# A paired-head recurrence on one core: the next pair's key projection moved behind the second inverse level, and one VectorE operation per chunk step

## The reference, cut to what matters

```python
zs = z + (jnp.pad(z, ((0, 0), (1, 0), (0, 0)))[:, :S] - z) * mu     # token shift
r, k, v, wd, ad, gd = _split(zs, ...)
w = -jax.nn.softplus(-(w0 + jnp.tanh(wd) @ w2)) - 0.5
decay = jnp.exp(-jnp.exp(w)); iclr = jax.nn.sigmoid(a0 + ad @ a2); g = jax.nn.sigmoid(gd) @ g2
kk = heads(k * k_k); kk = kk / jnp.maximum(jnp.sqrt(jnp.sum(kk * kk, -1)), 1e-12)
k = k * (1.0 + (iclr - 1.0) * k_a)
# per head, for each token:
#   sa = state @ a_t                       with a = -kk, b = kk * iclr
#   state = state * w_t + sa b_t^T + v_t k_t^T
#   y_t = state @ r_t
y = groupnorm(y) * gn_w + gn_b
bonus = jnp.sum(rh * kh * r_k, -1) * vh
out = (y + bonus) * g
```

## Time and profile before

| | us |
|---|---|
| median of three executions | 4002.56 |
| lowest, highest | 4001.58, 4009.13 |
| profiled execution | 4011.43 |
| its span, first to last instruction | 4009.6 |
| granted TensorE clock, mean | 0.984 |

### The profile page before, as it was taken

One profiled execution on the slowest core, in us unless ns is written; L12 is line 12 of the kernel. 1 busy time (PEld: TensorE's weight loads), 2 busy tenths in 40 slices (PEclk: granted clock), 3 DMA queues, 4 the chain that ended last, 5 costly groups with the idle time before them and its releaser, 6 DMA issues.

```text
span 4009.6 us, 68639 instructions
## 1 busy us (share of the span) xinstructions
PE 3778.5 (94%) x28412; PEld 3042.1 (76%) x28412; DVE 2020.4 (50%) x3578; ACT 1698.7 (42%) x2505; POOL 800.9 (20%) x1120
## 2 busy tenths in 40 slices
PE   7989999998999999989999999998999999999997
PEld 5777788777778877877777788876777777778885
DVE  4585651247553127356663476225645565357603
ACT  3475332346533237455553332235744544342223
POOL 1112222211222221200001222221120000222221
PEclk9999999999999999999999999999999999999998
DMA  9946998984699975733324889986583222779896
GB/s 306 232 97 141 278 243 188 234 216 106 137 208 194 192 171 114 178 86 69 69 61 98 176 189 192 193 176 143 114 183 74 54 63 53 158 172 192 191 193 139
DMA packets 191750, 628.90 MB, mean 157 GB/s; under 512 B 22992, under 2 KB 28368, under 8 KB 191056
## 3 DMA queue, kind: packets, MB, share of 16 engines
q0 software_dynamic: 160704, 549.53, 63.0%
q1 hardware_dynamic: 28176, 70.79, 5.1%
q10 hardware_dynamic: 2560, 4.20, 0.4%
HBM read 612.89 MB, written 2.10 MB: 153 GB/s over the span
## 4 chain that ended last, share of the span: by engine, by line
PE 51%; DVE 6%; DMA 3%; ACT 2%; issue 1%; SPq 0%; POOL 0%; DVEq 0%; ACTq 0%
PE bank L229 13%; PE bank L231 12%; PE bank L230 12%; PE bank L2091 4%; PE bank L2054 1%; DVE rw_z L2552 1%; PE bank L1772 1%; PE bank L1754 1%; PE bank L1745 1%; PE bank L2080 1%; DMA at_sw<-at_raw 1%; ACT gate L2280 1%; DMA w_lo<-in_b_wup 1%; DVE x L398 0%; PE bank L2068 0%
## 5 line engine op out<-in xcount | busy, mean ns | idle before, releaser
L229 PE MATMUL bank<-h_hi,w_hi 128*128 128x512 f32 x2608 | 1066.8, 409 | 25.8 <-DMA w_lo<-in_a_wgv 6.4
L231 PE MATMUL bank<-h_hi,w_lo 128*128 128x512 f32 x2608 | 1023.7, 393 | 0.0
L230 PE MATMUL bank<-h_lo,w_hi 128*128 128x512 f32 x2608 | 1023.1, 392 | 0.0
L162 ACT ACTIVATE w_lo<-w_hi 128x1024 fp32r<-128x1024 f32 (+2 forms) x558 | 557.6, 1003 | 1034.0 <-DMA w_hi<-in_a_wgv 292.7
L229 PEld LDWEIGHTS bank<-h_hi,w_hi 128*128 128x128 f32 x2608 | 493.8, 189 | 166.1 <-issue 52.5
L230 PEld LDWEIGHTS bank<-h_lo,w_hi 128*128 128x128 f32 x2608 | 494.1, 189 | 106.3 <-issue 11.5
L231 PEld LDWEIGHTS bank<-h_hi,w_lo 128*128 128x128 f32 x2608 | 493.4, 189 | 106.9
L2280 ACT ACTIVATE gate<-bank 128x512 f32<-128x512 f32 x96 | 57.3, 597 | 230.6 <-PE bank L2091 228.4
L1509 DVE TENSOR_SCALAR fa_conv<-fa_a_in,par_a 128x512 f32<-128x512 f32 x44 | 22.3, 507 | 228.9 <-ACT fa_a_in L1449 228.5
L229 PE MATMUL bank<-fa_y_hi,w_hi 128*128 128x512 f32 x352 | 137.1, 390 | 0.4 <-DMA w_lo<-in_a_wd 0.4
L229 PE MATMUL bank<-fb_y_hi,w_hi 128*128 128x512 f32 x352 | 137.0, 389 | 0.4 <-DMA w_lo<-in_b_wd 0.4
(11 more groups left out here) (466 smaller groups left out, 7505.0 us busy)
## 6 DMA issues: line engine op xcount, KB each, us to landing
w_hi<-in_a_wgv POOLq DMA_DIRECT2D x80, 512.0 KB, 5.3
w_lo<-in_a_wgv POOLq DMA_DIRECT2D x80, 512.0 KB, 7.6
w_hi<-in_b_wup POOLq DMA_DIRECT2D x80, 512.0 KB, 5.0
w_lo<-in_b_wup POOLq DMA_DIRECT2D x80, 512.0 KB, 7.4
w_hi<-in_a_wh POOLq DMA_DIRECT2D x48, 512.0 KB, 5.6
w_lo<-in_a_wh POOLq DMA_DIRECT2D x48, 512.0 KB, 5.6
w_hi<-in_b_wrkv POOLq DMA_DIRECT2D x48, 512.0 KB, 4.3
w_lo<-in_b_wrkv POOLq DMA_DIRECT2D x48, 512.0 KB, 5.4
```

What stands on the lines that cost most here:

```text
L162: st.do(st.eng.activation(self.lo[:, s], self.hi[:, s].bitcast(F32), ACT.Copy, scale=-1.0), (self.neg_made, n + 1))
L229: pe.matmul(out, self.hi[:, a], hh[:, k0 + k, :], start=first and k == 0, stop=False)
L230: pe.matmul(out, self.hi[:, a], hl[:, k0 + k, :], start=False, stop=False)
L231: mm = pe.matmul(out, self.lo[:, a], hh[:, k0 + k, :], start=False, stop=last and k == ks - 1)
```

## The change

Pieces change their place in the lists of the three engines; no operation is added or removed.

- PE: the k unit of pair p+1 stands in one piece behind `inverse_t(p, 1)` and its chunk step; the decay matmuls of pair p+1 stand in the last level, behind `lower(p, 4)` and its step. `dense(p)` begins with r; `ssq` stands behind its second block (behind its sixth in pair 0), the variance behind its fifth. The bonus matmul and `scores(p, 1)` stand behind `scores(p, 0)`, ahead of the four-way scores, each with chunk steps around them. The upper four-way products go to bank 4 instead of 3.
- ACT: the squares of the keys follow the decays; `keep_y` follows them; the variance's logarithm follows that of the key norm, so that both use one table load; k is copied in level 2 of the pair ahead. The weights of the pieces are negated in the same order, three calls at other places.
- DVE: the key shift stands in the pair ahead, between steps 21 and 22; `post` behind `at`; step 0 ahead of `rt`; and the operations up to level 1 are spread so that mostly one stands between two steps. The v shift is split in two around step 1.
- z: the buffer of a shift is chosen by `staged`.

```diff
@@ order of the banks @@
-            wide = [("w", p, 2, p_free), ("a", p, 5, p_free)]
-            order += wide if p else []
+            x, y = (0, 1) if p else (1, 0)
+            order += [("k", p, x, p_free), ("w", p, 2, p_free), ("a", p, 5, p_free), ("ssq", p, 3, pd_free)]
             if p >= 2:
                 order.append(("var", p - 2, 4, pn_free))
...
+            order += [("r", p, y, p_free), ("v", p, x, p_free), ("g", p, y, p_free), ("bonus", p, x, pd_free),
+                      ("t0", p, y, p_free), ("t1", p, x, p_free), ("t2", p, y, p_free)]
...
+        def staged(f):
+
+            q, i = (f - 3) // 3, (f - 3) % 3
+            return f % 2 if f < 6 else (q + i // 2) % 2
@@ PE, dense @@
+                def sums(k):
+                    if k == (1 if p else 5):
+                        pe.wait_ge(sq_made, p + 1)
+                        if p:
+                            pe.wait_ge(cx_kept, 5 * p)
+                        whole("ssq", p, bones[:, :], e0, ssq_made)
+                    if k == 4 and p >= 2:
                         pe.wait_ge(ysq_made, p - 1)
                         pe.wait_ge(xt_made, 6 * p)
                         whole("var", p - 2, bones[:, :], yq[:, :], var_made)
...
                 if p == 0:
-                    decays()
-                ws.project(pe, claim("r", p), hh, hl)
-                if p:
-                    key_norm()
-                ws.project(pe, claim("v", p), hh, hl, between=lambda k: key_norm() if p == 0 and k == 2 else None)
+                    ws.project(pe, claim("k", p), hh, hl)
+                    decays(p)
+                ws.project(pe, claim("r", p), hh, hl, between=sums)
+                ws.project(pe, claim("v", p), hh, hl)
...
@@ PE, the loop over pairs @@
                 scores(p, 0)
                 chain_on()
+                pe.wait_ge(rk_made, p + 1)
+                whole("bonus", p, bones[:, :], kp, bon_made)
+                scores(p, 1)
+                chain_on()
                 for first, last in ((0, 3), (3, 6), (6, 8)):
                     scores_four(p, first, last)
                     chain_on()
                 turned(p, 0)
                 chain_on()
-                scores(p, 1)
-                chain_on()
...
                 for i in range(LEVELS_):
                     lower(p, i)
                     chain_on()
                     if i < 2:
                         turned(p, i + 1)
                         chain_on()
+                    if i == LEVELS_ - 1 and more:
+                        decays(p + 1)
                     if i < LEVELS_ - 1:
                         inverse(p, i)
                     chain_on()
                     inverse_t(p, i)
                     chain_on()
+                    if i == 1 and more:
+                        claim("k", p + 1)
+                    if i == 1:
+                        key_blocks(KD)
@@ ACT @@
                 if p:
                     decays(p)
+                    square()
                     if p >= 2:
-                        log_var(p - 2)
-                        rstd(p - 2)
+                        keep_y(p - 2)
                     first_exps(p)
-                    ws.high(st, n + 2)
-                    copy_out("k", p, f, n)
+                    act.preload_act_table_set(LN_EXP)
...
                 do(e0, cum, ACT.Exp, signal=(eb_made, p + 1))
+                if p >= 2:
+                    log_var(p - 2)
+                    rstd(p - 2)
                 act.preload_act_table_set(TANH_EXP)
-                ws.high(st, n + 3)
+                if p:
+                    copy_out("r", p, f + 1, n + 1)
+                ws.high(st, n + 2)
                 copy_out("v", p, f + 2, n + 2)
...
                 do(mabt, banks[2][:, :], ACT.Copy, signal=(ab_made, p + 1))
+                ws.high(st, n + 3)
                 ws.high(st, n + 4)
...
                     if i < 2:
                         keep_turned(i + 1)
+                    if i == 2 and p + 1 < PAIRS:
+                        copy_out("k", p + 1, f + 3, n + 3)
@@ DVE, behind at @@
+                if p >= 2:
+                    post(p - 2)
+                shift(f + 1, "r", p, r, col("mu_r", p))
+                do(dve.scalar_tensor_tensor(out=kp, in0=r, scalar=col("r_k", p), in1=kp, op0=ALU.mult, op1=ALU.mult),
+                   (rk_made, p + 1))
+                step(0)
                 dve.wait_ge(eb_made, p + 1)
                 do(dve.tensor_tensor(rt[b], r, e0, ALU.mult), (rt_made, p + 1))
-                step(0)
-                shift(f + 2, "v", p, v, col("mu_v", p))
...
+                dve.wait_ge(*read("v", p))
+                shift_sub(f + 2, v)
                 step(1)
+                shift_add(f + 2, v, col("mu_v", p))
+                step(2)
+                keep_mrb()
+                step(3)
                 do(dve.tensor_copy(ec[:, b, :], e0[:, C - 1:S:C]))
                 ends = ec[:, b, :].unsqueeze(2).broadcast_to([P, NC, C])
                 do(dve.tensor_tensor(chunks(e0), chunks(a), ends, ALU.mult), (bbar_made, p + 1))
-                step(2)
+                step(4)
+                keep_low(0)
+                step(5)
+                first_x()
+                step(6)
+                dve.wait_ge(bon_made, p + 1)
+                do(dve.tensor_tensor(bonus[:, b, :], bank("bonus", p)[:, :], v, ALU.mult), read("bonus", p))
+                step(7)
                 first_xt()
-                step(3)
-                keep_low(0)
-                first_x()
-                step(4)
+                step(8)
                 keep_low(1)
-                step(5)
-                keep_mrb()
-                step(6)
-                step(7)
-                do(dve.tensor_tensor(chunks(e1), chunks(kt), ends, ALU.mult), (kbar_made, p + 1))
-                step(8)
                 add_x(0)
                 step(9)
                 add_xt(0)
-                step(10, 11)
+                step(10)
+                do(dve.tensor_tensor(chunks(e1), chunks(kt), ends, ALU.mult), (kbar_made, p + 1))
+                step(11)
...
-                step(20, 21, 22)
+                step(20, 21)
+                if p + 1 < PAIRS:
+                    keys(p + 1)
+                step(22)
                 add_xt(4)
                 step(23)
```

More of the change, by code:

```diff
@@ L2145, in scores @@
                 else:
-                    pe.wait_ge(x_made, LEVELS_ * p + 1)
+                    pe.wait_ge(rt_made, p + 1)
+                    pe.wait_ge(*read("ssq", p))
                     for c in range(NC):
@@ L2155, in scores_four @@
                 if first == 0:
-                    pe.wait_ge(rt_made, p + 1)
-                    pe.wait_ge(*read("ssq", p))
                     pe.wait_ge(*read("a", p))
+                    if p:
+                        pe.wait_ge(xt_made, 6 * p)
+                    if p >= 2:
+                        pe.wait_ge(*read("var", p - 2))
                 for c in range(first, last):
@@ L2166, in scores_four @@
                     for s_, o_ in crossed:
-                        up = pe.matmul(banks[3][o_, cut(c)], at_[b][s_, cut(c)], a[s_, cut(c)], start=True, stop=True)
+                        up = pe.matmul(banks[4][o_, cut(c)], at_[b][s_, cut(c)], a[s_, cut(c)], start=True, stop=True)
                     if c % 4 == 3:
@@ L2207, in inverse_t @@
                 pe.wait_ge(xt_made, 6 * p + i + 1)
-                if i == 0:
-                    pe.wait_ge(*read("bonus", p))
                 products(4, pp, xt[p % 2], xcxt_made)
@@ L2231, in _, with key_blocks @@
                 chain_on()
-                scores(p, 1)
-                chain_on()
+                more = p + 1 < PAIRS
+                ahead = ws.blocks(pe, banks[0][:, :], hh, hl) if more else None
+                def key_blocks(count):
+                    for _ in range(count if more else 0):
+                        next(ahead)
                 for i in range(LEVELS_):
@@ L2284, in copy_out @@
                 act.wait_ge(*ws.done(n + 1))
-                if f >= 2:
+                if 2 <= f < 6:
                     act.wait_ge(z_free, f - 1)
-                do(z[:, f % 2, 1:S + 1], bank(name, p)[:, :], ACT.Copy, signal=read(name, p))
+                elif f >= 6 and f % 3 < 2:
+                    act.wait_ge(z_free, f)
+                do(z[:, staged(f), 1:S + 1], bank(name, p)[:, :], ACT.Copy, signal=read(name, p))
             def keep_y(p):
@@ L2336, in _, with square @@
                 n, f = 3 + 3 * p, 3 + 3 * p
-                if p >= 2:
-                    keep_y(p - 2)
+                def square():
+                    if p:
+                        act.wait_ge(tr_made, 3 * p)
+                    act.wait_ge(z_free, f + 1)
+                    do(e0, ks, ACT.Square, scale=col("k_k", p), signal=(sq_made, p + 1))
                 if p:
                     decays(p)
+                    square()
                     if p >= 2:
-                        log_var(p - 2)
```

(24 more changed lines are left out.)

69 lines of the change are left out of this document (23 added, 46 removed).

## The result

| | before | after |
|---|---|---|
| median, us | 4002.07 (4 runs beside it) | 4032.34 (4 runs) |
| lowest to highest | 4000.84 to 4009.13 | 4024.79 to 4033.51 |
| profiled execution, its span | 4011.43, 4009.6 | 4033.51, 4031.7 |
| granted clock, mean | 0.984 | 0.982 |

The ratio is 1.0068, with an interval of 1.0051 to 1.0085: the change costs about 27 us, where 17.5 us less was forecast, and it lies above the top of the range (4004). It is slower, and not by the mechanism that the prediction had named for that side.

What follows compares the result with a forecast made beforehand. PE was taken as the bound, busy 94% of the span. Per stage 14.35 and 4.2 us gained, 8.8 and 1.0 lost: 8.75; two stages, 17.5 us, off the median 4002.56 give 3985 us, range 3967 to 4004.

Steps and rivals of the forecast that it cites:

- Step 1: Key unit moved behind `inverse_t(1)`: hides nothing there, 0.1 us charged per pair; negations and weight transfers priced at nothing.
- Step 2: Decay matmuls moved into the last level of the pair ahead cover a stop: 0.55 us gained, 0.9 before pair 1.
- Step 3: At the earlier `ssq` in r, PE waits for ACT's square: 1.2 us lost per pair, 1.6 in pair 1.
- Step 4: DVE and ACT in the dense part, shortened to 15.7 us: DVE in time with 0.5 us spare, cost nothing.
- DVE is late at step 0: Rival, chance 0.12 (slower): DVE's chain in the shortened dense part delays the first chunk-step copies; 10 us lost, 4012.
- Step 5: Between step 0 and level 2, the new order takes 18.33 us instead of 20.48: 2.15 us gained per pair.
- Step 6: Pair 0: PE idles 4.2 us at `ssq`, then half clock for 3.4 us; on average 1.0 us lost per stage.
- The gain of a pair: Net gain of each pair as the rivals quoted it: 1.45 us.
- the idle time only moves: Rival, chance 0.19: no matmul is removed, a pair gains 0.1 us and pair 0 costs 2; 3998 to 4004.
- new waits for DMA on the key weights: Sign that the forecast is wrong: PE newly waiting for transfers of the key weights; no size given.

Runs made afterwards that it cites:

- e5: The light after: the changed kernel, weight transfers from pair 1's r unit to the last pair carrying 64 of 1024 columns; ratio 1.0015, 4011.32 us.
- e12: e8 with the weight transfers from pair 1's r unit to the last pair cut to 64 of 1024 columns; ratio 0.9945, 3983.18 us.
- e8: e2 with pair 0's key sum back behind the third block of v; ratio 0.9995, 4003.04 us.
- e10: e9 with the decay matmuls back at the front of their own pair; ratio 0.9969, 3991.13 us.
- e9: The changed kernel, key unit back in its own pair, key sum behind v's second block (third in pair 0); ratio 0.9954, 3983.39 us.
- e2: The changed kernel with the key sum two blocks later in r for pairs 1 to 7; ratio 1.0014, 4009.78 us.
- e11: The changed kernel unaltered, run once more; ratio 1.0066, 4029.12 us.

## Why the prediction was wrong, by its steps

The sum had 8.75 us gained per stage; the profile has 8.3 and 10.2 lost: 17 and 19 us off. Of these 7.6 and 9.1 go away with light transfers: the fetches. The rest is what the light after shows against the forecast (484.3 and 483.3 against 483.6 - 8.75 = 474.9 and 482.2 - 8.75 = 473.5; 9.4 and 9.8, of which 1.6 and 0.9 are still "issue").

- **Step 1 failed, and it is the largest error.** It said that the weights are negated "some 20 us before use, and POOL's transfers keep their order", and priced that at nothing. Their order was kept; their place against PE's work was not. It looked for who waits for the weights (nobody does) and not for what the transfers hinder: PE's own instruction fetches, which started up to 4.78 us behind the crossing and made 18.0 us of stops. e5 against after, and e12 against e8, put that at about 20 us. The move of the unit on PE itself was right: 5.68 us from its start to the next `lower` against 5.56.
- **Step 2 about right.** The stop was covered; the decays ahead are worth 6 to 8 us of the whole (e10 against e9) where 2 x 4.2 was forecast.
- **Step 3 right.** The key sum goes 5.05 us behind the decay matmuls, as worked out, and PE stood 0.97 to 1.33 for it, mostly 1.04, forecast 1.2: 7.4 us in the first stage for 8.8. e2 shows what it was worth, and that the stop was not needed: two blocks later there is none.
- **Step 4 right.** DVE was in time for step 0. Its timeline in pair 4, the bonus factor, then the copy at step 0, which waits for PE and not PE for it:

```profile
1947.25 0.75 DVE L2552 SCALAR_TENSOR_TENSOR gate<-gate,par_b 128x512 f32<-128x512 f32 x1
1949.02 0.23 DVE L2462 COPY rw_rhs<-bank 128x64 f32<-128x64 f32 x1 [1.02 <-PE bank L2071]
```

  So the rival "DVE is late at step 0", on which the whole chance of slower stood, did not occur.
- **Step 5 was mis-sized.** From step 0 to level 2, without a stop marked "issue", it takes 19.0 us and not 18.33: a gain of 1.48 a pair for 2.15. The stop of 1.36 went as planned; more small ones than placed remained, at step 5, `turned` and the inverse's copies. With three further misses (step 0 at 18.30 behind the decays for 18.02, the key unit 5.68 for 5.56, the levels 10.42 for 10.28) a light pair takes 53.35 where 52.19 was forecast, 7.0 us over six intervals.
- **Step 6 was mis-sized.** The stop came, 3.96 for 4.2:

```profile
1724.87 1.22 PE L2056 MATMUL bank<-w,rw_bones 128*128 128x512 f32 x1 [3.96 <-ACT w L2288]
```

  The lower clock followed it, as forecast, and in both stages; but it held 6.8 us, twice what was assumed (in e5, behind the same stop, 6.8 and 3.4). From pair 0's decays to its inverse(0) it was 0.8 and 3.1 us longer than before, for a forecast of 0.2 and 1.9: on average 1.9 us a stage for 1.0. e8 shows that none of this is needed.

The gain of a pair, 1.45 in the prediction's rivals, is 1.40 by the terms of its own sum (2.15 - 0.1 - 1.2 + 0.55); nothing hangs on it. The rival "the idle time only moves" came nearest: without the fetches the kernel would be at 1.0015 to 1.0022. The list of what would prove the forecast wrong had "new waits for DMA on the key weights"; the transfers did it, by another way.

What stays open: what in the DMA engines holds a fetch's start back, and why a stop falls in some pairs and not in others. A steady pair has 1882 of PE's instructions, 7.35 blocks, so that the borders stand elsewhere in each pair; that this decides was not tried. The two profiles differ by less than the ratio says: 18.5 us in the stages and 3.5 in the rest of the span. That before's profiled run stands 9.4 us above the median of its runs, and after's 1.2, makes up for most of it; the rest of the span goes up to 15 us apart between other profiles.

## What to carry to other kernels

A transfer that nobody waits for still has a price, if it falls into a stretch where an engine goes through its instructions fast: before a dense stretch is shortened, or a negation that releases a transfer is moved, look where in PE's program the transfers will run, and keep them under the large matmuls. Stops that end with "issue" on an engine whose operands are ready ask for the DMA queue of the instructions. The distance of its packets alone doesn't tell: before has fetches with up to 391 instructions between them and no stop, after has stops behind 294. What tells is whether each stop stands at a block's border and ends just behind a packet's landing. And a new order is worth taking apart: here the new middle order and the decays ahead gave 18 us, while the early key sum, pair 0 and the key unit's traffic took 45.

## What the runs showed of the hardware

- One fetch of PE's instructions is a 16 KB packet for 256 of them and takes about 1 us. It starts 0.48 us (median, before) behind PE's crossing into the last block that it has, so that PE has 256 instructions in hand. Among 64 x 64 products these last mostly 4.2 to 4.9 us. With weight transfers holding 92% of the DMA engines' time (186 GB/s) the fetch started 3.63 us behind the crossing, landed, and PE went on 1.61 us later, after a stop of 1.36.
- The Trainium skill (Runtime: NRT & Kernel Launch, Instruction fetch mechanics) gives PE's store as 2048 instructions. By that figure, as an estimate, eight blocks would be in hand and a fetch that is 4.78 us late would be harmless. The same section of the Trainium skill also says that the store is only two blocks, with the 32 KiB of the other engines beside it. At all 111 stops PE had used up every block landed before and waited for the next, so the measurement decides: two blocks are in play, not eight.
- Behind PE's idle 3.96 us the granted clock was 0.50 for 6.8 us, in both stages of after; in e5, behind 3.97 us, for 6.8 and 3.4 us; in e11, behind 1.62 and 1.94 us, for 3.4 us.
